# Five gate products made during compression, x loaded turned, and a reordered end of the projections, in a kernel for one hybrid attention and MoE layer

## The reference, cut to what matters

```python
h = rmsnorm(x)                       # x * rsqrt(mean(x*x)) * norm1_g
u, q, qm, kvc, kvs, kvw, gn, gb = split(h @ w_in)
# pool input 256, NSA queries 512, memory queries 256, three k/v groups of 256,
# 24 head gates, and gb: one gate per branch and output channel, 3 x 1024
A = pool_mix(u)                      # causal means of 2/4/8/16 tokens, small matmuls
B = gn0*cmp_attn + gn1*selected_attn + gn2*window_attn
C = cross_attention(qm, memory)      # 256 memory rows: rmsnorm(mem) @ w_mem_kv
x = x + (sum_b sigmoid(h @ w_gb[b]) * (branch_b @ w_up[b])) @ w_out
x = x + moe(rmsnorm(x))              # top 4 of 32 experts
```

## Time and profile before

| | |
|---|---|
| median of 3 runs | 1881.05 us (1879.68 to 1882.05) |
| the profiled execution | 1884.05 us, its span 1882.2 us |
| mean granted TensorE clock | 0.945 of full speed |
| busy: PE / PEld / DVE / ACT / POOL | 1724.1 / 965.1 / 546.0 / 335.9 / 454.5 us |
| TensorE's share of the span | 92% |
| moved by DMA | 535.93 MB, 285 GB/s over the span |

### The profile page before, as it was taken

One profiled execution on the slowest core, in us unless ns is written; L12 is line 12 of the kernel. 1 busy time (PEld: TensorE's weight loads), 2 busy tenths in 40 slices (PEclk: granted clock), 3 DMA queues, 4 the chain that ended last, 5 costly groups with the idle time before them and its releaser, 6 DMA issues.

```text
span 1882.2 us, 40022 instructions
## 1 busy us (share of the span) xinstructions
PE 1724.1 (92%) x16122; PEld 965.1 (51%) x16122; DVE 546.0 (29%) x1347; ACT 335.9 (18%) x736; POOL 454.5 (24%) x522
## 2 busy tenths in 40 slices
PE   7997876688799999969999999999999999999992
PEld 3545762444588886533556673444443434343431
DVE  2222014266111111372323232323232322222226
ACT  3232222255200000111111111111111111111110
POOL 1113547377100001411222212121222222222220
PEclk9997976789799999969999999999999999999996
DMA  8207877540431103057999999999999999999986
GB/s 303 102 31 224 308 199 224 168 175 1 151 116 56 52 27 117 23 210 307 424 425 413 425 423 413 424 426 417 425 414 414 424 426 421 413 421 420 420 363 244
DMA packets 84179, 535.93 MB, mean 285 GB/s; under 512 B 19601, under 2 KB 43633, under 8 KB 71154
## 3 DMA queue, kind: packets, MB, share of 16 engines
q1 hardware_dynamic: 63065, 493.83, 65.2%
q0 software_dynamic: 14544, 32.03, 5.0%
q10 hardware_dynamic: 6512, 9.33, 1.4%
HBM read 518.72 MB, written 28.39 MB: 291 GB/s over the span
## 4 chain that ended last, share of the span: by engine, by line
PE 53%; DVE 1%; DMA 0%; issue 0%; POOLq 0%; POOL 0%; ACT 0%; SPq 0%
PE psum L2874 35%; PE psum L2900 18%; DVE arena L2856 1%; PE psum L2884 0%; DVE arena L2864 0%; DMA arena<-y_of 0%; DMA y_of<-arena 0%; DMA arena<-scr_h,arena 0%; DVE arena L2807 0%; POOL arena L2744 0%; POOLq L2675 0%; ACT arena L2793 0%; POOLq L2748 0%; POOLq L2744 0%; POOLq L2750 0%
## 5 line engine op out<-in xcount | busy, mean ns | idle before, releaser
L2874 PE MATMUL psum<-arena 128*32 128x512 f32 x6144 | 668.0, 592 | 2.8 <-issue 2.8
L2874 PEld LDWEIGHTS psum<-arena 128*32 128x32 f32 x6144 | 234.6, 108 | 416.8 <-issue 413.2
L2900 PE MATMUL psum<-arena 128*32 128x256 f32 x6144 | 344.8, 378 | 0.0
L2900 PEld LDWEIGHTS psum<-arena 128*32 128x32 f32 x6144 | 235.9, 109 | 110.1 <-issue 10.4
L2829 DVE TENSOR_TENSOR arena<-psum,arena 128x512 f32<-128x512 f32 x96 | 66.5, 692 | 592.1 <-PE psum L2874 592.1
L2761 POOL DMA_INDIRECT y_of<-arena x96 | 96.9, 1010 | 471.6 <-ACT arena L2793 471.6
L2505 PE MATMUL psum<-arena 128*128 128x272 f32 x768 | 184.0, 398 | 1.8 <-PEq L231 1.8
L2505 PEld LDWEIGHTS psum<-arena 128*128 128x128 f32 x768 | 147.7, 192 | 35.9 <-issue 3.4
L2789 ACT ACTIVATE arena<-arena 128x256 f32<-128x256 f32 x96 | 40.1, 418 | 610.1 <-DVE arena L2831 610.1
L2740 POOL DMA_INDIRECT arena<-scr_h,arena x96 | 99.5, 1036 | 49.3 <-POOL arena L2736 28.5
L799 PE MATMUL psum<-arena 128*128 128x512 f32 (+1 forms) x256 | 90.1, 510 | 0.2 <-DVE arena L660 0.2
(11 more groups left out here) (364 smaller groups left out, 1473.5 us busy)
## 6 DMA issues: line engine op xcount, KB each, us to landing
arena<-in_w_gu SPq DMA_DIRECT2D x64, 4096.0 KB, 14.6
arena<-in_w_down SPq DMA_DIRECT2D x32, 4096.0 KB, 14.1
arena<-in_w_gb SPq DMA_DIRECT2D x24, 512.0 KB, 3.5
arena<-y_of SPq DMA_DIRECT2D x8, 1024.0 KB, 13.7
...
arena<-in_x_all SPq DMA_DIRECT2D x8, 512.0 KB, 11.3
```

Of the source, the lines that this page charges most:

```text
L2874: mm = pe.matmul(gu_bank(g)[32 * j:32 * j + 32].rearrange("p (h n) -> p h n", h=2), xgT[:, g, 32 * k:32 * k + 32], gu_w(slot)[:, part, :, ...
L2900: mm = pe.matmul(dn_half(g)[32 * j:32 * j + 32], actT[:, g, 32 * k:32 * k + 32], dn_w(slot)[:, part, 256 * j:256 * j + 256], start=(k == 0 ...
```

## The change

It has seven parts.

1. *x comes turned.* The function that lays out the inputs adds `x_turned`, each tile transposed. SP loads it beside x (4 KB per partition and tile) into the place of `xn`, ahead of all else, and `w_tok`'s first chunk in two halves behind it. TensorE's 56 transposes of x and memory are gone. Tile 0 is multiplied unnormed (gain only, `gained`) and ScalarE applies the reciprocal root while it copies the product out; `rooted` scales tile 0 of `hT` afterwards for later readers. For tiles 1 to 6 the roots are put on a diagonal and spread over all partitions by one product with ones (`spread_root`), and VectorE makes `hT` from the turned x, the gain and the spread roots in 8 operations per tile. ScalarE squares tiles 0 to 3 before its first copy and 4 to 6 after it.
2. *Five gate weights in x's place.* When all rows have been squared, SP loads the `w_gb` of units 19 to 23 into x's place (`fill_w`).
3. *Projections' end reordered.* The memory products go to banks 3 and 4 and wait for `s_ze` 15, not 19. The pool-input products follow `project(6)` at once, then history turns, heads, the position term's products (moved here from compression), the 55 small products, the eight tables in a row, all copied by ScalarE, row turns, `w_pool`. The page row is computed early; the pages of sequence 0 are loaded after tile 4's products (POOL's gathers too), those of sequence 1 after memory's.
4. *Later joins.* SP no longer waits for the landing of tables and pool rows at the end of the stage; the waits stand in compression (ScalarE before its constant loads at s = 0 and s = 1, SP and POOL before the selected pages).
5. *Gate products in compression.* After `keys(s-1)` for s = 1 to 5 TensorE makes the gate product of one of those units in banks 0 and 1; VectorE copies it to `fill_out`, ScalarE stores it raw to `scr_gate` at s + 1. `hT`'s spill moves to s = 4, memory loads to one each at s = 2 to 5, window loads to s = 6.
6. *Prompt attention* takes its groups tile by tile, (memory, compressed, selected, window) for tiles 3 to 0, in a ring of four.
7. *Gate stage.* For units 19 to 23 SP loads the stored product in place of the weights, ScalarE takes the sigmoid from SBUF, TensorE makes the up product alone, VectorE waits for both.

```diff
--- before
+++ after
+    turned = np.zeros((NT + 2, 128, D), np.float32)
+    for n, rows in enumerate([f["x_all"][128 * t:128 * t + ROWS[t]] for t in range(NT)] + [f["mem"][0:128], f["mem"][128:256]]):
+        turned[n, :, 0:KD * len(rows)] = rows.reshape(len(rows), KD, 128).transpose(2, 1, 0).reshape(128, -1)
+    f["x_turned"] = turned
...
+root_bank = lambda n: bank(1 if n in (2, 3) else 0)[:, 128 * (n % 4):128 * (n % 4) + rows_of(n)]
...
+FILL = 5
+FIRST_FILL = 24 - FILL
+fill_w = x.rearrange("p n d -> p (n d)")[:, 0:FILL * KD * 128].rearrange("p (j k n) -> p j k n", j=FILL, k=KD)
+scr_gate = scratch("scr_gate", [FILL, 128, NTOK])
...
+            sp.dma_start(xT[:, n % 2, 0:KD * r], i["x_turned"][n, :, 0:KD * r]).then_inc(s_xT[n], 16)
...
+        sp.dma_start(gain_cols, i["gain_cols"]).then_inc(s_gc, 16)
+        load_turned(0)
+        for half in range(2):
+            q = slice(4 * half, 4 * half + 4)
+            sp.dma_start(w_tok[:, q, 0:512], w[:, q, 0:512]).then_inc(s_wtok[0] if half else s_wt0, 16)
         load_x(0)
...
+        load_turned(1)
+        load_w_tok(1)
...
+        for c in range(2, 4):
+            load_w_tok(c)
...
         for n in range(2, 7):
             load_x(n)
+        for n in range(2, 4):
+            load_turned(n)
         sp.dma_start(w_mem, i["w_mem"].rearrange("(k p) n -> p k n", p=128)).then_inc(s_wmem, 16)
         sp.dma_start(w_u, i["w_u"].rearrange("(k p) n -> p k n", p=128)).then_inc(s_wmem, 16)
+        sp.dma_start(page_list, i["page_list"].partition_broadcast(128).rearrange("p a n -> p (a n)")).then_inc(s_pg, 16)
...
+        load_turned(4)
+        sp.wait_ge(s_root, 7)
+        for j in range(FILL):
+            u = FIRST_FILL + j
+            sp.dma_start(fill_w[:, j], i["w_gb"][u // 3, u % 3].rearrange("p (k n) -> p k n", k=KD)).then_inc(f_w, 16)
...
+        def pages_and_constants():
+            sp.wait_ge(s_zp, 20)
+            sp.dma_start(inv_count, i["c_inv_count"].rearrange("p (k t) -> p k t", k=2)).then_inc(s_pl, 16)
+            sp.dma_start(w_pool, i["w_pool"].rearrange("k p n -> p k n")).then_inc(s_pl, 16)
+            sp.dma_start(hist[0:120], i["state_pool"].rearrange("s t c -> (s t) c")).then_inc(s_pl, 16)
+            sp.dma_start(w_cmp, i["w_cmp"].rearrange("p (c j m) -> p c j m", c=2, j=8)).then_inc(s_cw, 16)
...
+            sp.wait_ge(s_ix, 1)
+            load_sub(sp, 0, range(0, 10))
...
+            if n < 2:
+                load_turned(5 + n)
+            if n == 2:
+                pages_and_constants()
+        sp.wait_ge(s_zp, 22)
+        load_sub(sp, 1, range(0, 10))
...
-            if h in BY_DVE:
-                sp.wait_ge(s_td, BY_DVE.index(h) + 1)
-            else:
-                sp.wait_ge(s_ta, by_act(h))
+            sp.wait_ge(s_ta, h + 1)
             sp.dma_start(scr_desc[h].rearrange("(p m) -> p m", p=128), table[h]).then_inc(s_tw, 16)
-            load_sub(sp, 1, range(h + h // 3, h + 1 + (h + 1) // 3) if h < 7 else range(9, 10))
...
-        sp.wait_ge(s_uo, 32)
-        sp.wait_ge(s_tw, 16 * NH)
...
+                if n == 0:
+                    act.wait_ge(s_xn, 1)
+                    act.activation(zt[0:r, 0, a:b], bank(2 + c)[0:r, 0:b - a], ACT.Copy, scale=rinv[0:r, 0:1]).then_inc(s_ze, 1)
...
+            act.activation(zm[:, m], bank(3 + m), ACT.Copy).then_inc(s_ze, 1)
...
+        for n in range(4):
+            mean_square(n)
         for n in range(NT):
             evacuate(n)
+            if n == 0:
+                for m in range(4, 7):
+                    mean_square(m)
...
+        evacuate_mem(0)
+        heads_out(NT - 2)
+        evacuate_mem(1)
+        roots(NT)
+        pooled(0, 0)
+        pooled(0, 1)
+        roots(NT + 1)
+        pooled(1, 0)
+        pooled(1, 1)
+        act.wait_ge(s_ht, 2)
...
                            ACT.Copy).then_inc(s_he, 1)
+        heads_out(NT - 1)
+        for m in range(2):
+            keys_out(m)
...
+        act.activation(bias_cmp_p.rearrange("p h m -> p m h"),
...
+        for r in range(2):
+            q = slice(64 * r, 64 * r + 64)
+            act.activation(pe_bias[q, :], bank(3)[q, 8 * SHIFTS:8 * SHIFTS + 4].rearrange("p (c r) -> p r c", r=2)[:, r],
+                           ACT.Copy).then_inc(s_pbe, 1)
...
+        for h in range(NH):
+            table_out(h)
...
+            if n == 0:
+                dve.wait_ge(s_const, 48)
+            dve.tensor_scalar(diag[0:r, n % 4, 0:r], ident[0:r, 0:r], rinv[0:r, n:n + 1], None, ALU.mult).then_inc(s_xn, 1)
+
+        def gained(n):
+            dve.wait_ge(s_xT[n], 16)
+            dve.wait_ge(s_gc, 16)
+            dve.tensor_tensor(dstT(n), xT[:, n % 2].rearrange("p (k t) -> p k t", k=KD),
+                              g1c.unsqueeze(2).to_broadcast([128, KD, 128]), ALU.mult).then_inc(s_hT, 1)
...
+        def rooted(n):
+            dve.wait_ge(s_zp, 4)
+            dve.wait_ge(s_tp, n + 1)
+            dve.tensor_tensor(dstT(n), dstT(n), root_bank(n).unsqueeze(1).to_broadcast([128, KD, 128]),
+                              ALU.mult).then_inc(s_fix, 1)
...
+            dve.wait_ge(s_tp, (2, 2, 4, 4, 7, 7, 7)[n])
+            dve.wait_ge(s_xT[n], 16)
+            for k in range(KD):
+                ins = dve.scalar_tensor_tensor(dstT(n)[:, k], xT[:, n % 2, r * k:r * k + r], g[:, k:k + 1],
+                                               root_bank(n), ALU.mult, ALU.mult)
+            ins.then_inc(s_hT, 1)
...
+        gained(0)
+        for n in range(2):
             norm(n)
+        to_hT(1)
+        for n in range(2, 4):
+            norm(n)
+        rooted(0)
+        for n in range(4, 7):
+            norm(n)
+        dve.wait_ge(s_pg, 16)
+        dve.tensor_scalar(page_row, page_list, float(PAGE), cols[:, 0:1], ALU.mult, ALU.add).then_inc(s_ix, 1)
+        for n in range(3, 7):
             to_hT(n - 1)
...
+            if n == NT:
+                pool.wait_ge(s_zp, 20)
+                pool.wait_ge(s_ix, 1)
+                gather_sub(pool, 0)
...
+            pe.wait_ge(s_hT, n + 1)
...
+                        pe.wait_ge(s_wtok[c] if c else s_wt0, 16)
...
+                        if n == c == 0 and k == KD // 2:
+                            pe.wait_ge(s_wtok[0], 16)
...
+                    for m in {(0, 0): (0, 1), (1, 0): (2, 3), (1, 3): (4, 5, 6)}.get((n, c), ()):
+                        spread_root(m)
...
-                pe.wait_ge(s_ze, 19)
+                pe.wait_ge(s_ze, 15)
...
         project(6)
+        pe.wait_ge(s_ze, 20)
+        for k in range(2):
+            for h in range(2):
+                for kk in range(KD):
+                    mm = pe.matmul(u_bank(k, h)[:, 0:HALF], w_u[:, kk, k * 128:k * 128 + 128],
+                                   hT[:, kk, h * HALF:(h + 1) * HALF], start=(kk == 0), stop=(kk == KD - 1))
...
+        pe.wait_ge(s_ze, 22)
+        pe.wait_ge(s_pl, 48)
+        for k in range(2):
...
+        pe.wait_ge(s_cw, 48)
+        for c in range(2):
+            for j in range(8):
+                pe.matmul(bank(3)[:, 8 * SHIFTS + 2 * c:8 * SHIFTS + 2 * c + 2], w_cmp[:, c, j], pe_cmp[:, c, j],
+                          start=(j == 0), stop=(j == 7))
+        pe.wait_ge(s_oh, 32)
+        pe.wait_ge(s_r97, 2)
+        for m in range(SHIFTS):
+            at = 16 * (SHIFTS - 1 - m)
+            mm = pe.matmul(bank(3)[:, 8 * m:8 * m + 8], asc_b[0:97, at:at + 128], rel_parts[0:97],
...
-                pe.wait_ge(s_ta, by_act(h - 2))
+            if h >= 2:
+                pe.wait_ge(s_ta, h - 1)
...
+        pe.wait_ge(s_te, 22)
+        pe.wait_ge(s_ue, 8)
+        for h in range(NH):
+            bias_table(h)
...
+        pe.wait_ge(s_bce, 1)
+        pe.wait_ge(s_pbe, 2)
+        pe.wait_ge(s_he, 4)
...
-        sp.dma_start(scr_hT, hT.rearrange("p k t -> p (k t)")).then_inc(s_spill, 16)
...
+            if s == SPILL_AT:
+                sp.dma_start(scr_hT, hT.rearrange("p k t -> p (k t)")).then_inc(s_spill, 16)
...
+        sp.wait_ge(s_tw, 16 * NH)
+        sp.wait_ge(f_s, 16 * FILL)
+        sp.wait_ge(s_uo, 32)
...
+        pool.wait_ge(s_tw, 16 * NH)
+        pool.wait_ge(f_s, 16 * FILL)
...
+                act.wait_ge(s_uo, 32)
...
+                act.wait_ge(s_tw, 16 * NH)
...
+            if 2 <= s < FILL + 2:
+                act.wait_ge(f_e, 2 * (s - 1))
+                act.dma_start(scr_gate[s - 2], fill_out[:, s - 2]).then_inc(f_s, 16)
+            if 2 <= s < 6:
+                load_memory(act, 0, s - 2)
+            if s == FILL + 1:
                 act.wait_ge(s_spill, 16)
                 for n in range(4):
...
             after(s)
+            if s < FILL:
+                for h in range(2):
+                    dve.wait_ge(f_p, 2 * s + h + 1)
+                    dve.tensor_copy(fill_out[:, s, HALF * h:HALF * h + HALF], bank(h)[:, 0:HALF]).then_inc(f_e, 1)
...
-        for c in range(2):
-            for j in range(8):
-                mm = pe.matmul(bank(7)[:, 2 * c:2 * c + 2], w_cmp[:, c, j], pe_cmp[:, c, j],
```

(35 more changed lines are left out.)

217 lines of the change are left out of this document (73 added, 144 removed).

## The result

The changed kernel takes 1864.12 us (median of 4 runs, 1863.31 to 1865.46) against 1881.55 for the kernel before in the same runs: ratio 0.9906, interval 0.9891 to 0.992. So it is faster, by 17.4 us, but the forecast was 1849.3 and the time lies 2 us above the range. The profiled execution has a span of 1861.7, 20.5 under the 1882.2 of before; I had 31.7. All that follows accounts for the 11.2 between them.

What follows compares the result with a forecast made beforehand. TensorE was taken as the busiest engine in every stage, so only its idle time and work leaving it could be won. The terms summed to -31.7 us, giving a median of 1849.3 us, range 1838 to 1862.

Steps and rivals of the forecast that it cites:

- A: Start of projections: first product at 7.2, second chunk landing at 18.5, tile 1 earlier; -4.7 us (bounds -8 and +1).
- B: Projections: x's transposes for tiles 3 to 6, about 1 us each, go and five root products come; -2.5 us.
- C: Projections: memory's product waits for bank 3 only, evicted long before; -1.35 us.
- F: Projections' tail: 32 two-column products and table copies in a row, against waits filled; net +2.0 us (bounds -3 and +8).
- D: Drain from projections into compression: pages out earlier, landings awaited later, 8.2 shrinks to 1.1; -7.1 us (bounds -8 and -3).
- E: Start of compression: the 32 two-column position-bias products leave; -7.0 us.
- G: Compression: five gate products add 37.0, page hole filled, first-keys wait not; net +28.7 us (bounds +37 and +22.8).
- H: Prompt attention: memory tiles between tiles, four buffers, longest POOL wait stays; -2.4 us (bounds -12 and +6).
- I: Gate stage: five products of 7.33 go, last unit's sigmoid wait too; -37.3 us (bounds -34 and -37.5).
- compression gives nothing back: Rival, compression: queues issue no faster and waits reappear elsewhere, +37; total about 1857.6 us; chance 0.12.
- gates at half rate: Rival, compression: TensorE stalls before all five gate products and slows, some 12 us lost; 1861 us; chance 0.06.
- rival with late stored gates: Rival, gate stage: last five units each wait for a read, eating the stage's gain; +5.6, 1886.6 us; chance 0.03.

Runs made afterwards that it cites:

- Experiment 1: On the changed kernel: head transposes of tiles 0 and 1 earlier, 1863.84 us; gate weights issued after the output stores, 1859.78; both, 1856.79.
- eight kernels counted there: Changed kernel and follow-up runs, compared on the 64 records ending with tile 1's first chunk: four took 22.66 us, four 24.25 to 24.36.
- experiment 8: Two-column products moved behind second pool-input product, on experiment 6's base: 1850.24 us; moved back to compression's start, on experiment 6's kernel: 1844.06 us.
- experiment 7: SP again waits for tables and pool rows at projections' end, on experiment 6's base: 1847.82 us.
- experiment 6: Gate products stored earlier, on Experiment 1's both plus second w_tok chunk first, its root product later, first gate product before first keys: 1847.20 us.
- experiment 5: Prompt attention's order and ring of three as before the change, on Experiment 1's run with both edits: 1860.19 us.
- experiments 4: Two gate products moved to compression instead of five, on Experiment 1's run with both edits: 1856.95 us.
- their base: The changed kernel with both edits of Experiment 1, head transposes earlier and gate weights later: 1856.79 us.

## Why the prediction was wrong, step by step

By the timelines of TensorE, predicted and found, in us:

| step | predicted | found |
|---|---|---|
| A: start of tile 1 | -4.7 | -1.0 (38.9 to 37.9) |
| B and C: from there to the second memory product | -3.85 | +1.8 (89.1 to 90.9) |
| F: from there to the end of `w_pool` | +2.0 | +2.5 (40.5 to 43.0) |
| D, drain | -7.1 | -6.0 |
| E, position term | -7.0 | -6.9 |
| G, compression | +28.7 | +27.0 (96.7 to 123.7) |
| join into decode | 0 to 1 | +2.1 |
| decode | 0 | -0.2 |
| H, prompt attention | -2.4 | -3.4 (120.9 to 117.5) |
| I, gate stage | -37.3 | -39.2 (246.5 to 207.2) |
| output product to experts; experts | 0 | +2.1; +0.7 |
| sum | -31.7 | -20.5 |

- **A and B failed**, and make 9.3 of the 11.2 (3.7 and 5.6; C's wait of 1.35 is gone as forecast). B took x's transposes as 1 us each that leaves. The row behind them in the old trace was the clue: between the head transposes and the next tile stood one transpose group, and ScalarE evicted underneath it. With the cover gone TensorE waits for that eviction; removing the transposes wins next to nothing for tiles 3 and 4 (1.0 goes, 0.83 and 1.15 come). "The stores are needed two tiles later, so nothing" was the second half of it: it counted the tiles but not that SP's queue can stand still for 20.8 us. Experiment 1 shows both: its two edits together give 5.0 of the 5.6 back. A was mis-sized in three places: the first product came at 8.3 and not 7.2, the second chunk at 20.6 and not 18.5, and 1.7 of slow clock followed the wait for it, as in half of the eight kernels counted there; the 8.7 for the first chunk was right.
- **F's sum was right, in part by luck; E right but nearly empty.** I took 4.2 us for the 32 records in the tail; they took 5.28 (4.0 to 6.8 in other runs). Of the waits of 2.17 and 0.57 that I took as filled, 0.70 and 0.56 stand again behind the pool-input products, and the tables ran at 0.61 where they had 0.38. Against that the pool-input products in one row took 14.7 in place of 16.3, which I had not counted. Of E's 7.0 the records alone took 5.3 back here, and undoing E costs nothing that the totals show (experiment 8).
- **D was near in size (6.0 of 7.1), half wrong in reason.** I named both "pages go out earlier" and "the landings are awaited later". With the pages early, the second is worth nothing (experiment 7).
- **G was right in mechanism**: the page hole filled, the first-keys hole not, the first gate slow by 1.7. The rivals "compression gives nothing back" and "gates at half rate" fall: gates two to five took 7.50 each. The 0 to 1 for the fifth store was 2.1. I had the right engine, POOL's 16 gathers, but reckoned that the join comes when they end; it comes 5.5 us later (experiment 6).
- **H and I came out a little above the forecast, partly by luck.** H's named waits for POOL gave 2.1 and not 3.3 (1.44, 2.03 and 2.61 became 1.09, 1.25 and 1.62), the long one grew by 1.0, and the 2.4 more that I set against them at the start did not come. By undoing it H is worth 3 to 6 us (experiment 5). From the third unit on, I gave 36.9; the other 2.3 lie in the first two units, which the change doesn't touch and which were slower in the old trace. The rival with late stored gates fell: the units ran without a wait. None of the three signs of being wrong that the prediction named came: the wait that broke it, for an eviction, was not among them.
- Most of the 2.1 behind the gate stage is one row: the output product took 29.43 us in place of 27.73 behind a wait of about 2 us that both kernels have. It took 27.74 in experiments 4 and 5 and 29.43 in their base. What decides that is open.
